# Second layer's attention: the weights' scaling on GpSimd in place of VectorE

## What is computed

```python
def sink_probs(s, sinks):
    sk = sinks.astype(jnp.float32).reshape(SW_KV_HEADS, SW_GROUP)[..., None, None]
    mx = jnp.maximum(jnp.max(s, axis=-1, keepdims=True), sk)
    p = jnp.exp(s - mx)
    return p / (jnp.sum(p, axis=-1, keepdims=True) + jnp.exp(sk - mx))

# swa_prompt: q, k, v in blocks of 128; kc, vc = the block before and this one
    s = jnp.einsum('bnqkgd,bnskd->bnkgqs', qb, kc).astype(jnp.float32) * (SW_HD ** -0.5)
    s = jnp.where(mask[None, :, None, None], s, -jnp.inf)
    p = sink_probs(s, sinks).astype(v.dtype)
    o = jnp.einsum('bnkgqs,bnskd->bnqkgd', p, vc).reshape(B, T, SW_HEADS * SW_HD)
```

## Time and profile before

| | |
|---|---|
| median of 3 runs | 1376.63 us (1376.25 to 1376.86) |
| profiled execution, own time | 1378.69 us |
| its span | 1376.9 us |
| TensorE busy | 1349.7 us, 98% |
| VectorE busy | 876.9 us, 64% |
| ScalarE busy | 572.7 us, 42% |
| GpSimd busy | 33.4 us, 2% |
| first scores of the attention, last weighing | 801.5 us, 869.6 us |

### The profile page before, as it was taken

One profiled execution on the slowest core, in us unless ns is written; L12 is line 12 of the kernel. 1 busy time (PEld: TensorE's weight loads), 2 busy tenths in 40 slices (PEclk: granted clock), 3 DMA queues, 4 the chain that ended last, 5 costly groups with the idle time before them and its releaser, 6 DMA issues.

```text
span 1376.9 us, 25708 instructions
## 1 busy us (share of the span) xinstructions
PE 1349.7 (98%) x11039; PEld 1303.7 (95%) x11039; DVE 876.9 (64%) x1616; ACT 572.7 (42%) x1024; POOL 33.4 (2%) x57
## 2 busy tenths in 40 slices
PE   7999999999999999999999989999999999999998
PEld 6999978999999999999999966999999999999998
DVE  5536677687777775222896579668777777522386
ACT  4222245554444443222753147555444444322372
POOL 2000100000000000000010000000000000000000
PEclk9999999999999999999999999999999999999999
DMA  8321641212323333222332220231232233323231
GB/s 260 109 92 62 214 139 62 93 47 77 93 92 92 91 91 132 85 87 77 138 108 89 81 70 15 78 93 47 78 92 93 92 93 93 128 86 105 62 135 63
DMA packets 34498, 131.91 MB, mean 96 GB/s; under 512 B 4212, under 2 KB 4684, under 8 KB 34112
## 3 DMA queue, kind: packets, MB, share of 16 engines
q1 hardware_dynamic: 29520, 112.49, 25.2%
q0 software_dynamic: 4864, 17.78, 4.1%
HBM read 121.61 MB, written 10.05 MB: 96 GB/s over the span
## 4 chain that ended last, share of the span: by engine, by line
PE 87%; DVE 8%; ACT 3%; issue 1%; DMA 1%; SPq 0%; DVEq 0%; ACTq 0%
PE tile L942 22%; PE tile L946 22%; PE tile L944 22%; PE tile L952 4%; PE tile L953 4%; PE tile L954 4%; DVE wL L1492 1%; DVE sm L2114 1%; DMA raw<-in_w_kv 1%; DVE cv L1517 1%; PE side L1411 1%; PE sums L1429 1%; DVE soft L2129 1%; PE side L1349 1%; ACT wH L548 1%
## 5 line engine op out<-in xcount | busy, mean ns | idle before, releaser
L548 ACT ACTIVATE wH<-raw 128x1024 fp32r<-128x1024 f32 (+1 forms) x192 | 212.9, 1111 | 428.4 <-DMA raw<-in_w_up 141.5
L942 PE MATMUL tile<-xH,wH 128*128 128x260 f32 x1840 | 375.1, 285 | 12.2 <-DVE xL L1576 8.5
L946 PE MATMUL tile<-xH,wL 128*128 128x260 f32 x1840 | 372.4, 284 | 0.0
L944 PE MATMUL tile<-xL,wH 128*128 128x260 f32 x1840 | 371.9, 284 | 0.0
L1492 DVE TENSOR_TENSOR wL<-raw,wH 128x1024 fp32r<-128x1024 f32 (+1 forms) x192 | 247.9, 1291 | 151.0 <-ACT wH L548 146.7
L942 PEld LDWEIGHTS tile<-xH,wH 128*128 128x128 f32 x1840 | 285.6, 190 | 16.5 <-issue 12.4
L946 PEld LDWEIGHTS tile<-xH,wL 128*128 128x128 f32 x1840 | 285.6, 190 | 0.0
L944 PEld LDWEIGHTS tile<-xL,wH 128*128 128x128 f32 x1840 | 284.9, 190 | 0.0
L1532 DVE TENSOR_TENSOR u<-tile,rstd 128x520 f32<-128x520 f32 x96 | 67.1, 699 | 144.8 <-PE tile L946 144.8
L942 PE MATMUL tile<-hidH,wH 128*128 128x260 f32 x616 | 124.3, 283 | 0.0
L946 PE MATMUL tile<-hidH,wL 128*128 128x260 f32 x616 | 123.9, 283 | 0.0
(11 more groups left out here) (365 smaller groups left out, 1868.5 us busy)
## 6 DMA issues: line engine op xcount, KB each, us to landing
raw<-in_w_up SPq DMA_DIRECT2D x88, 512.0 KB, 3.6
raw<-in_w_down SPq DMA_DIRECT2D x32, 704.0 KB, 4.0
raw<-in_w_ple SPq DMA_DIRECT2D x16, 512.0 KB, 5.6
raw<-in_w_kv SPq DMA_DIRECT2D x12, 512.0 KB, 3.8
raw<-in_w_qo SPq DMA_DIRECT2D x12, 512.0 KB, 3.6
raw<-in_w_qkv SPq DMA_DIRECT2D x12, 512.0 KB, 3.6
cring<-in_c_in POOLq DMA_DIRECT2D x8, 512.0 KB, 4.5
out_c_s<-cring POOLq DMA_DIRECT2D x8, 512.0 KB, 3.3
```

What stands on the lines that cost most here:

```text
L548: nc.scalar.activation(wH[j][:, 0:n], raw[j][:, 0:n], ACT.Copy).then_inc(s_high, 1)
L942: nc.tensor.matmul(out[:, q, 0:HT], wh, x[0][:, k, tokens(q)], start=first, stop=False)
L944: nc.tensor.matmul(out[:, q, 0:HT], wh, x[1][:, k, tokens(q)], start=False, stop=False)
L946: mm = nc.tensor.matmul(out[:, q, 0:HT], wl, x[0][:, k, tokens(q)], start=False, stop=last)
```

## The change

VectorE's `normalise` becomes `denominators`: sum and inverse, and then `s_wden` counts up. The four multiplies move to GpSimd with the same operands, in a loop over the 16 groups that waits for `s_wden` and counts `s_norm` up. The loop stands behind the stores of k_p and v_p; the store of v_s moves behind group 6 and that of k_s behind group 8; the loads of `convw` and `prev` now come behind group 15 in GpSimd's program. All waits on `s_norm` stay as they were.

```diff
@@ gpsimd
-                    pool.wait_ge(s_qp, 1)
-                    pool.dma_start(g.k_s, kc[:, :, :, 1:WINDOW + 1]).then_inc(s_out, 16)
-                    pool.wait_ge(s_vtr, 3)
-                    pool.dma_start(g.v_s[WINDOW - 1], vnew[:]).then_inc(s_out, 16)
+
+                    def normalise(gi):
+
+                        k, w0 = gi % 2, P if gi < 4 else 0
+                        pool.wait_ge(s_wden, gi + 1)
+                        for c in range(4):
+                            last = nc.gpsimd.tensor_scalar(soft[:, k, c, w0:], soft[:, k, c, w0:], sm[:, k, 3, c:c + 1],
+                                                           None, ALU.mult)
+                        last.then_inc(s_norm, 1)
+
+                    for gi in range(4 * NB):
+                        normalise(gi)
+                        if gi == 6:
+                            pool.wait_ge(s_vtr, 3)
+                            pool.dma_start(g.v_s[WINDOW - 1], vnew[:]).then_inc(s_out, 16)
+                        if gi == 8:
+                            pool.wait_ge(s_qp, 1)
+                            pool.dma_start(g.k_s, kc[:, :, :, 1:WINDOW + 1]).then_inc(s_out, 16)
@@ vector
-            def normalise(gi):
+            def denominators(gi):
                 k = gi % 2
-                w0 = P if gi < 4 else 0
                 dve.wait_ge(s_soft, gi + 1)
                 chain.link(nc.vector.tensor_tensor(sm[:, k, 3, :], sm[:, k, 3, :], sm[:, k, 2, :], ALU.add))
-                chain.link(nc.vector.reciprocal(sm[:, k, 3, :], sm[:, k, 3, :]))
-                for c in range(4):
-                    last = nc.vector.tensor_scalar(soft[:, k, c, w0:], soft[:, k, c, w0:], sm[:, k, 3, c:c + 1], None,
-                                                   ALU.mult)
-                last.then_inc(s_norm, 1)
+                nc.vector.reciprocal(sm[:, k, 3, :], sm[:, k, 3, :]).then_inc(s_wden, 1)
@@ vector, the loop over the groups
-                normalise(gi)
+                denominators(gi)
```

More of the change, by code:

```diff
@@ L311, in build @@
         s_sig, s_side = sem("sigmoid_done"), sem("side_read")
-        s_psq = sem("ple_square")
+        s_psq, s_wden = sem("ple_square"), sem("denominator_ready")
         s_out, s_ystored = sem("stored"), sem("y_stored")
```

## The result

The changed kernel took 1405.71 us (median of 4 runs, 1404.81 to 1408.83) against 1376.74 for the kernel before on the same chip: ratio 1.0209, 95% interval 1.0195 to 1.0223, 29 us slower. The forecast had the direction, and its range held the time; its size was +12.2 us.

What follows compares the result with a forecast made beforehand. TensorE was taken to bound at 3.67 us a group, VectorE nearly as full. Loop +7.7, reload +4.0 and end +0.5 made +12.2 us on 1376.63, so 1388.8 us; range 1374 to 1450.

Steps and rivals of the forecast that it cites:

- the term N: Time of GpSimd's four multiplies of 128x256 in one attention group, taken as 2.3 us, with break-even at 1.53.
- the loop through both engines: Attention groups: inverse, GpSimd's multiplies, maximum two groups on, next inverse in a row; 4.55 us a group, +7.7 over ten steps.
- The bound and the cap: Attention: TensorE cannot go under 3.67 us a group; freeing VectorE of the multiplies gains at most some 3 us.
- rival B: GpSimd slow at arithmetic, four multiplies 3.2 to 7 us or more: 1418.5 at 5, 1440 at 7; chance 0.20, above 7 0.12.
- N over 3.2: Sign of being wrong: GpSimd's four multiplies of an attention group taking longer than 3.2 us.
- The ISA row: Reload ahead of GpSimd's first multiply, from 808.66 us, taken as 5 us and holding up group 0; counted +4.0 us.
- Groups 0 to 3: Short attention groups with 128x128 weights: about 3.5 us each against 3.71 before, so no change either way.
- The end: Group 15, last of the attention: weights turned at 867.33 against 866.60 us, less 0.2 for VectorE's earlier copy; +0.5 us.
- The stores and the loads behind them: GpSimd's queue: v_s and k_s fit in its idle time, convw and prev come early enough; cost 0, stores up to 0.7 us.
- rival C: TensorE's new gaps in the attention keep its clock at the lower level: +28 us, 1409 with the reload; chance 0.06.
- a changed length there: Sign of being wrong: anything outside 803 to 885 us changing its length.
- N near 1.0: GpSimd's four multiplies at the skill's roughly line-rate; the prediction put its sum 3 us lower then.

Runs made afterwards that it cites:

- N = 4.53: Changed kernel plus a fifth GpSimd multiply of the same shape, of a constant into scratch, in groups 0 to 14: 1418.66 us, ratio 1.0292.
- the two-factor kernel: Changed kernel with a second factor 1.0 in GpSimd's multiply, four multiplies taking 1.84 us: 1382.58 us, ratio 1.0029.
- the one with two heads and two places: Changed kernel with VectorE scaling two heads, GpSimd two with second factor 1.0, two places for the small columns: 1377.06 us, ratio 1.0002.
- with four places: Changed kernel with four places instead of two for the small columns (shift, sums, inverse), GpSimd's multiplies unchanged: 1389.76 us, ratio 1.0083.

## Why the prediction was right in kind and wrong in size

The step that failed is the term N, the time of GpSimd's four multiplies: the sum had 2.3 us, and the chip took 3.63. The mechanism, the loop through both engines, was as forecast. The ten steps from group 4 to group 14 start and end with these rows in the kernel before:

```profile
822.45 1.14 DVE L2129 TENSOR_SCALAR soft<-soft,sm 128x256 f32<-128x256 f32 x4
...
860.43 1.14 DVE L2129 TENSOR_SCALAR soft<-soft,sm 128x256 f32<-128x256 f32 x4
```

Point by point, in the order of the prediction:

- **The bound and the cap.** Right in size: with the multiplies nearly gone, TensorE's 3.65 us a group bounds and the attention is 2.7 us shorter; with the work divided and four places it is 3.1 shorter.
- **The loop through two engines.** Right in every link. The experiments with N = 4.53 and 1.84 follow it at the same 2.10, and opening the loop takes 1 us a group away. Its fixed part was taken as 2.25 and is 2.10: GpSimd answers VectorE in 0.09 us, not 0.29. The 0.29 of the earlier trace rows was the start of a DMA issue (the store of k_p, too, starts 0.29 us after the rotation's end, 805.79 for 805.50), and the multiplies start sooner.
- **N, the term that failed.** I took 2.3 us, 0.55 a multiply, as twice the memset's rate. It is 3.63. A multiply with one factor costs 0.27 us fixed (I had 0.10) and 2.5 ns an element (I had 1.76). The choice "nearer to the memset since that is the same engine" rested on nothing that the trace showed; the same engine does a two-factor multiply at the memset's rate and the one-factor one at a third of it. Ten steps from group 4 to group 14 went from 37.98 us to 58.18 (GpSimd's rows at 824.85 and 883.03): +20.2, forecast +7.7. Put into my own sum, N = 3.63 gives (2.25 + 3.63 - 3.78) x 10 = +21.0. The miss in the middle is this one figure; rival B held it, with a chance of 0.20, and "N over 3.2" was one of the signs of being wrong. Why the one-factor form is the slow one stays open.
- **The ISA row.** Wrong. I charged 4.0 us and the first multiply starts at 807.07, before the row of the store of v_p has ended (807.21). At most its first four multiplies are slower, 2.60 for 2.35. The reload's own two rows take 0.30 us each and overlap the store's. The Trainium skill's 6 us for a freshly loaded routine ("GPSIMD Engine Reference", Instruction dispatch) does not appear here.
- **Groups 0 to 3.** Wrong, and it made up by luck for the term before: I had "nothing", but from the rotation's end to group 4's multiplies it took 15.48 us before and 19.35 after, +3.9. These are the short groups' own multiplies, 2.35 us for four of 128x128 where I had about 1.3. My 3.71 us a group of before was also a mean that hid the first steps: group 0's multiplies to group 1's took 2.39 us and the next step 2.71, against 4.17 and 3.91 after. Reload and short groups together were forecast +4.0 and came to +3.9 for another reason.
- **The end.** Forecast +0.5, measured +1.9 (group 14's multiplies to the first `sout` product: 9.09 us before, 11.02 after). N again, and the last eight multiplies take 7.74 us where twice 3.63 is 7.26: VectorE's subtractions of `x_low_att` run beside them, and one of the eight takes 1.43 us for 0.92.
- **The stores and the loads behind them.** Right: v_s and k_s lie in GpSimd's idle time (1.55 and 1.03 us of it are left ahead of the groups behind them), the groups do not come later for them.
- **The clock, rival C.** It did fall, to 0.85 on average over the ten groups, which I had thought unlikely, but it decided little there: the groups kept the 5.73 us of the loop at either level. Only between groups 5 and 6 were they 6.00 apart, with VectorE waiting 3.35 us for TensorE's scores while the clock was 0.50. Behind the attention it shows: `sout` took 33.88 us at a mean granted clock of 0.90, for 32.29 at 0.95. The forecast had nothing for that stage, and a changed length there was one of its signs of being wrong.
- **The Trainium skill on the rate.** "Roughly line-rate" for one input ("GPSIMD Engine Reference", Engine selection) is what the two-factor form shows in its 0.84 ns an element, apart from its fixed 0.25 us; the one-factor form, which this kernel uses, shows 2.5 ns. At the 1.2 GHz that the Trainium skill gives for GpSimd ("GPSIMD Engine Reference", Specifications) these are, as estimates, one cycle and three. The prediction's remark that N near 1.0 would put the sum 3 us lower is wrong by its own formula: 2.25 + 1.0 lies under TensorE's 3.67, so the ten steps give -1.1 in place of +7.7 and the end 0.7 less, some 9 us lower.

In sum: 20.2 + 3.9 + 1.9 = +26.0 us in the attention, +1.6 behind it and -1.5 ahead of it, the 26.1 of the pair.

The length of the `sout` stage goes with TensorE's granted clock over it. TensorE is busy through all of the stage in each of the ten profiles: 30.79 us at 1.00 (the two-factor kernel), 32.29 to 32.41 at 0.95 (four kernels, before among them), 33.85 to 34.05 at 0.90 (five, the changed one and the one with two heads and two places among them). Executions of one kernel differ in the same way: the ten of the two-factor kernel took 1378.67 to 1380.10 us where the clock's mean over the span was 0.995 or 0.996, 1382.37 to 1382.89 at 0.993, and 1384.48 to 1385.23 at 0.991. Its profiled execution is one of the four quick ones. In other kernels the tie is looser: with four places 1389.30 us stands at 0.993 and 1389.83 at 0.995.

What stays open: what in or behind the attention decides whether the clock falls in the `sout` stage. The three lengths are 1.5 us apart and more, which is as much as the best version gains.

## What to carry to other kernels

Work moved to another engine is paid at its own time plus everything that was ordered behind it: look for the wait that was empty because the same engine served both sides (here a buffer's reuse, two groups on), since that wait turns the two engines into one loop in which neither runs beside the other. Work out the loop's fixed part from the trace first; it gives the duration from which the move loses (here 1.7 us for four multiplies), and where nothing in the trace shows that duration, measure it alone before anything else, in each form in which it can be written. More places for the small buffer opened the loop for 128 bytes a partition of SBUF, and dividing the heads between the engines was better than moving all of them.

## What the runs showed of the hardware that was not expected

- On GpSimd `x * s` with no second operation takes 0.91 us for 128x256, and `x * s * 1.0` takes 0.46. The slope is 2.5 against 0.84 ns an element, the fixed part 0.27 and 0.25.
- GpSimd started its multiplies 0.09 us after the end of the VectorE instruction that released them (848.55 to 848.64 in the changed kernel), and a DMA issue 0.29 us after (820.49 to 820.78 in the kernel before).
- A VectorE subtraction with two operands in SBUF (1.21 us) added 0.59 to 1.04 us to GpSimd multiplies beside it and was not slowed itself. VectorE's multiplies by a column and GpSimd's, started together, slowed each other, 0.84 for 0.62 and 1.12 for 0.93 us.
- With TensorE busy throughout, the same 252 products took 30.79 us at a mean granted clock of 1.00, 32.29 at 0.95 and 33.88 at 0.90; the difference between kernels in this one stage is as large as the best gain in the attention.
